# Second input projection, mLSTM cell and second output projection in one block of a two-part transformer kernel

## Chip, cores and metric

The kernel runs on one core of one Trainium2 chip. The metric is the device time of one execution in microseconds (us), as the median of several runs.

## The reference, cut to what matters

Two blocks follow each other on 256 tokens of width 2048, all in float32. The first (two kinds of attention) ends in `h`. The second starts with `layernorm`, then computes this, and ends with a mixture of experts over the result (`peer_ffn`), which is untouched here:

```python
proj = h @ w_in[l]
cB, cC, ch, q, k, v, o, gi, gf = jnp.split(proj, split_at, axis=-1)
y_conv = cB * causal_dwconv(cC * ch, conv_w[l], conv_b[l])
gates = (jnp.concatenate([gi, gf], axis=-1) + b_gate[l]).astype(jnp.float32)
logi = gates[..., :M_HEADS]
logf = jax.nn.log_sigmoid(gates[..., M_HEADS:])
hm = mlstm_chunkwise(hd(q), hd(k), hd(v), logi, logf)
hm = layernorm(hm, mh_norm_g[l].reshape(M_HEADS, M_HEAD_DIM), ...)
y_m = jax.nn.sigmoid(o) * hm.reshape(Bn, S, D_MLSTM)
mix = jnp.concatenate([y_conv, y_m], axis=-1) @ w_out[l]
h = layernorm(ALPHA * h + mix, ln1_g[l], ln1_b[l])
```

`cB`, `cC`, `ch`, `q`, `k`, `v`, `o` are 1024 wide each, `gi` and `gf` 8. The cell `mlstm_chunkwise` has 8 heads of width 128; for each it weighs `q k^T` by exponentials of the gates under a causal mask, multiplies with `v` and divides by a row sum.

## The kernel before

**Slabs.** Every weight matrix is read as slabs of 128 x 1024 float32 (512 KB). SP loads slab n into `raw[n % 4]` once slab n-4 has been split. ACT rounds it into `w_hi` (`round_slab`, L146, two halves of 512 columns), DVE writes the rest `w_lo = raw - w_hi` (`split_slab`, L153, two halves), and PE multiplies hi*hi, lo*hi and hi*lo (L162 to L164). `w_hi` and `w_lo` have two buffers each, so ACT may round a half of slab m once PE is through with that half of slab m-2. On ACT and on DVE the work of slab m+1 is written ahead of whatever belongs to slab m. `feature_slab` makes 24 products of 256 columns from a slab (features on the partitions), `token_slab` 12 of 512 columns (tokens on the partitions). Both wait on `lo_ready` for each half of their slab. Each engine runs its instructions in the order in which they are written; the engines meet only at semaphores.

**Three stages**, each a block of its own with a branch on every engine at its end (L64):

- The second input projection (from L1070): 8 transposes of `h` with rounding and splitting; 48 slabs for `cB`, `cC`, `ch`, six for each of 8 groups of 128 features, in a loop, with the convolution of a group as seven DVE instructions in a row (L1187 to L1199) behind the group's last split; 32 slabs for q and k in loops; the gate columns (L1114, L1118); then 32 slabs for v and o, written out without a loop for PE and ACT.
- The cell (from L1240): DVE, ACT and PE make the gates' running sums and maxima; GpSimd (POOL) copies each head's q and k into `qk` and multiplies `o2` with the norm's gain (L1254); then for each head PE makes the scores and the exponents' row (L1328, L1329, L1331), DVE masks (L1389, L1390), ACT takes exponentials (L1283 to L1285), DVE weighs (L1395), PE multiplies with v (L1341 to L1343), ACT copies the result out (L1290), DVE divides (L1407 to L1416). After the eighth head come the norm over all heads (L1428 to L1443), 16 transposes of `hm` (L1356), and their rounding and splitting into `mix_hi` and `mix_lo` (L1303, L1448). No slab is multiplied in this stage; SP loads none.
- The second output projection (from L1458): 32 slabs of `w_out_2`, `token_slab` in loops, with the residual sum after every 8 slabs (L1501), at the end the norm `norm_stats` (8 instructions L279) and `norm_apply` (L288, L289).

## Time and profile before

| | us |
|---|---|
| median of 3 runs | 3099.87 |
| lowest and highest | 3096.27, 3116.24 |
| the profiled execution, its own time | 3101.69 |
| its span in the trace | 3099.5 |

The profiled execution is 1.8 us above the median; 2.2 us lie outside its span. Over the span PE is busy 2911.5 us (94%), DVE 1670.1, ACT 1329.3, POOL 620.5. The three stages that are changed lie between 1013.6 and 1525.0 us of the span.

### The profile page before, as it was taken

How to read it: one execution, taken by the hardware profiler on the slowest of the kernel's cores; microseconds unless marked ns; L12 is line 12 of the kernel's file. 1: busy time of each engine (PE TensorE's matmuls, PEld its weight loads, DVE VectorE, ACT ScalarE, POOL GpSimd, SP SyncE). 2: the span in 40 equal slices, each digit the busy share in tenths (PEclk: the TensorE clock that was granted, in tenths of full speed). 3: DMA queues.
4: the chain of work that ended last, by engine and by line, in shares of the span. 5: the costliest groups of instructions: out<-in, count | busy, mean ns of one | idle time of the engine just before them, and what ended most of it. 6: DMA issues, size and time to landing. Idle time of an engine off the chain costs nothing.

```text
span 3099.5 us, 53380 instructions
## 1 busy us (share of the span) xinstructions
PE 2911.5 (94%) x16728; PEld 2535.3 (82%) x16728; DVE 1670.1 (54%) x3187; ACT 1329.3 (43%) x2492; POOL 620.5 (20%) x496
## 2 busy tenths in 40 slices
PE   8999998899887899987799999999999999999996
PEld 7987877888665899866699998888887888888885
DVE  3143245322456665446588875555555666666666
ACT  2132243322543444433344445555554555555553
POOL 1100001200000000010000187777751111111110
PEclk9999999999988899978899999999999999999998
DMA  7742355933343355424444567777767666666663
GB/s 271 276 135 89 96 164 159 366 102 98 102 150 135 138 189 191 167 83 157 160 166 175 176 176 184 185 188 185 185 192 249 215 216 218 219 218 218 215 214 131
DMA packets 182994, 554.19 MB, mean 179 GB/s; under 512 B 53776, under 2 KB 53808, under 8 KB 179600
## 3 DMA queue, kind: packets, MB, share of 16 engines
q1 hardware_dynamic: 136656, 500.25, 47.9%
q0 software_dynamic: 45696, 48.88, 7.2%
q10 hardware_dynamic: 576, 4.19, 0.3%
q8 instruction: 41, 0.67, 0.1%
q14 instruction: 25, 0.20, 0.0%
HBM read 532.13 MB, written 21.10 MB: 178 GB/s over the span
## 4 chain that ended last, share of the span: by engine, by line
PE 49%; DVE 1%; ACT 0%; issue 0%; ACTq 0%; DVEq 0%
PE PS L1706 11%; PE PS L162 11%; PE PS L163 10%; PE PS L164 10%; PE PS L1708 6%; PE PS L1677 0%; DVE stats L279 0%; DVE hb L1987 0%; PE PS L254 0%; DVE hb L289 0%; DVE hb L288 0%; DVE w_lo L153 0%; DVE wj_lo L1755 0%; DVE h L268 0%; ACT w_hi L146 0%
## 5 line engine op out<-in xcount | busy, mean ns | idle before, releaser
L153 DVE TENSOR_TENSOR w_lo<-raw,w_hi 128x512 fp32r<-128x512 f32 x1696 | 1177.8, 717 | 919.3 <-ACT w_hi L146 917.4
L146 ACT ACTIVATE w_hi<-raw 128x512 fp32r<-128x512 f32 x1696 | 1030.5, 629 | 924.0 <-PE PS L164 823.0
L1706 PE MATMUL PS<-h,w_hi 128*128 128x512 f32 x1504 | 533.1, 400 | 2.0 <-DVE w_lo L153 2.0
L1619 POOL DMA_INDIRECT g_dram<-gt,spot x256 | 418.1, 1633 | 454.4 <-DVE gt L1947 348.6
L1708 PE MATMUL PS<-h,w_lo 128*128 128x256 f32 x1504 | 423.2, 281 | 0.0
L162 PE MATMUL PS<-w_hi,wj_hi 128*128 128x512 f32 x1024 | 399.3, 390 | 4.3 <-DVE wj_lo L1755 4.3
L164 PE MATMUL PS<-w_hi,wj_lo 128*128 128x512 f32 x1024 | 398.8, 389 | 0.0
L163 PE MATMUL PS<-w_lo,wj_hi 128*128 128x512 f32 x1024 | 398.8, 389 | 0.0
L1706 PEld LDWEIGHTS PS<-h,w_hi 128*128 128x128 f32 x1504 | 283.4, 188 | 73.1 <-DVE w_lo L153 2.4
L1708 PEld LDWEIGHTS PS<-h,w_lo 128*128 128x128 f32 x1504 | 284.9, 189 | 0.0
L162 PE MATMUL PS<-h,w_hi 128*128 128x256 f32 x800 | 228.8, 286 | 5.0 <-DVE w_lo L153 2.9
L162 PEld LDWEIGHTS PS<-w_hi,wj_hi 128*128 128x128 f32 x1024 | 192.6, 188 | 45.0 <-DVE wj_lo L1755 3.9
L163 PE MATMUL PS<-h,w_hi 128*128 128x256 f32 x800 | 227.0, 284 | 0.0
L164 PE MATMUL PS<-h,w_lo 128*128 128x256 f32 x800 | 227.0, 284 | 0.0
L163 PEld LDWEIGHTS PS<-w_lo,wj_hi 128*128 128x128 f32 x1024 | 192.6, 188 | 39.9
L164 PEld LDWEIGHTS PS<-w_hi,wj_lo 128*128 128x128 f32 x1024 | 192.5, 188 | 40.1
L162 PE MATMUL PS<-x_hi,w_hi 128*128 128x256 f32 (+1 forms) x512 | 177.0, 346 | 22.5 <-ACTq L480 13.0
L1631 POOL TENSOR_TENSOR wt<-wt,pick 128x512 f32 (+1 forms) x64 | 82.6, 1291 | 533.0 <-PE PS L164 483.2
L162 PE MATMUL PS<-h_hi,w_hi 128*128 128x256 f32 x640 | 179.3, 280 | 4.2 <-DVE w_lo L153 2.5
L163 PE MATMUL PS<-h_lo,w_hi 128*128 128x256 f32 x640 | 178.2, 278 | 0.0
L164 PE MATMUL PS<-h_hi,w_lo 128*128 128x256 f32 x640 | 178.2, 278 | 0.0
L163 PE MATMUL PS<-x_lo,w_hi 128*128 128x256 f32 (+1 forms) x512 | 175.2, 342 | 0.0
(322 smaller groups left out, 4373.4 us busy)
## 6 DMA issues: line engine op xcount, KB each, us to landing
raw<-in_u_s SPq DMA_DIRECT2D x256, 512.0 KB, 4.1
raw<-in_v SPq DMA_DIRECT2D x256, 512.0 KB, 4.6
raw<-in_w_in_s SPq DMA_DIRECT2D x112, 512.0 KB, 3.6
raw<-in_w_mod_s SPq DMA_DIRECT2D x64, 512.0 KB, 4.6
raw<-in_w_in_a SPq DMA_DIRECT2D x64, 512.0 KB, 3.7
raw<-in_w_in_b SPq DMA_DIRECT2D x64, 512.0 KB, 3.7
raw<-in_w_out_s SPq DMA_DIRECT2D x64, 512.0 KB, 3.5
raw<-in_w_gate_s SPq DMA_DIRECT2D x32, 512.0 KB, 3.5
```

The costliest lines, as they stand in the source:

```text
L146: act.activation(w_hi[m % 2][:, half], raw[:, m % NRAW, half], ACT.Copy).then_inc(hi_ready, 1)
L153: dve.tensor_tensor(w_lo[m % 2][:, half], raw[:, m % NRAW, half], w_hi[m % 2][:, half].bitcast(F), ALU.subtract).then_inc(lo_ready, 1)
L162: pe.matmul(out, lhs[0], rhs[0], start=start, stop=False)
L163: pe.matmul(out, lhs[0], rhs[1], start=False, stop=False)
L164: return pe.matmul(out, lhs[1], rhs[0], start=False, stop=stop)
L1619: pool.indirect_dma_start(g_dram, bass.IndirectOffsetOnAxis(spot[:, t, h, k:k + 1], 0), gt[:, t, h, k:k + 1], None, compute_op=ALU.add).th ...
L1631: pool.tensor_tensor(two, two, pick[:, b, :].rearrange("p (j t) -> p j t", j=2), ALU.mult)\
L1706: pe.matmul(PS[:, 6 + j % 2, :], w_hi[m % 2][:, c], h_both[:, kk, :, :].rearrange("p a t -> p (a t)"), start=(kk == 0), stop=False)
L1708: last = pe.matmul(PS[:, 6 + j % 2, 0:T], w_lo[m % 2][:, c], h_hi[:, kk, :], start=False, stop=(kk == KT - 1))
```

## The change

The three stages become one block. The order of the slabs changes: q and k first (loops), then the gates, then v and o with the gates' running sums between their slabs, then the 48 convolution slabs, written out, and between them the cell, one head for each group of six slabs, then the output projection, written out. DVE's work for a group and a head is cut into pieces of one to six instructions, one behind each slab's split (`conv_first`, `conv_second`, `mask` with `conv_third`, `divide`, `weigh`, `centre`). The convolution's last two steps go to ACT (`mix_round`) and POOL (`mix_lo`); ACT also copies out `a_sb`. The scores read q and k straight from `q2` and `k2`, so POOL's copies are gone. The norm over a head's 128 values is taken head by head: `centre` subtracts the mean and multiplies with `o2` (now with the gain); the scale by the root of the variance is applied for all heads at once in the output projection, half on DVE, half on ACT. The output projection first takes, for three of the four column blocks, the slabs that need only the convolution's half of `mix` (12 slabs), and between its 9th and 11th slab come the 16 transposes of `hm`; then the other 12, then the 8 of the fourth block. The sums of the last norm are taken after each block of columns. ACT loads the table of Exp after the last o slab, and the table of Sqrt at the fifth output slab. `w_in_2` and `w_out_2` are laid out on the host in the new order; slabs, products and bytes are the same in number.

```diff
+        OUT2 = [(c, g) for c in range(3) for g in range(4)] + [(c, g) for c in range(3) for g in range(4, 8)] + [(3, g) for g in range(8)]
+        with stage() as blk:
+            @blk.sync
+            def _(sp):
+                load_slabs(sp, src_in2, base["in2"], NRAW, N_WIN2)
+                load_slabs(sp, src_out2, base["out2"], 0, NRAW)
+                load_slabs(sp, src_out2, base["out2"], NRAW, N_OUT2)
+                load_slabs(sp, src_wq, base["wq"], 0, NRAW)
+                sp.wait_ge(ready, 2)
+
+                sp.dma_start(h_dram, h_buf[:, :, :]).then_inc(h_stored, 16)
...
+                pool.wait_ge(par_in, 80)
+                pool.wait_ge(vo_free, 4)
+                pool.tensor_tensor(o2[:, :, :], o2[:, :, :], mh_g[:, None, :].broadcast_to([P, TT, WA]), ALU.mult).then_inc(o_gate, 1)
+                for e in range(HEADS):
+                    pool.wait_ge(mixed_hi, e + 1)
+                    pool.tensor_tensor(mix_lo[:, e, :], yc[:, e % 2, 1, :], mix_hi[:, e, :].bitcast(F), ALU.subtract)\
+                        .then_inc(mixed, 1)
+
+                pool.wait_ge(scores, HEADS)
+                for i, name in enumerate(("ln1_g", "ln1_b")):
+                    pool.dma_start(par[i][:, :], bcast(io[name])).then_inc(ln_in, 16)
```

PE between the v and o slabs, then heads beside slabs, then the output projection:

```diff
+                for c in range(4):
+                    if c >= 2:
+                        pe.wait_ge(vo_free, c - 1)
+                    for g in range(8):
+                        token_slab(pe, [PS[:, 2 * (c % 2) + t, :] for t in range(TT)], None, m0 + 32 + 8 * c + g, g, h_hi, h_lo)
+                        if (c, g) == (0, 4):
+                            pe.wait_ge(g_dve, 1)
+                            pe.wait_ge(acc_free, 2 * HEADS + 2)
+                            for a in range(2):
+                                for t in range(TT):
+                                    last = pe.transpose(PS[0:HEADS, 7, a * T + t * P:a * T + (t + 1) * P], lg[:, t, 4 * a, :], ident)
+                            last.then_inc(g_tr, 1)
...
+                def score(e):
+                    w = e % 2
+                    if e == 0:
+                        pe.wait_ge(vo_free, 4)
+                    if e >= 2:
+                        pe.wait_ge(wts, e - 1)
+                    q, k = q2[:, e, :], k2[:, e, :]
+                    pe.matmul(PS[:, w, 0:T], k[:, 0:P], q, start=True, stop=True)
+                    pe.matmul(PS[:, w, T:T + P], k[:, P:T], q[:, P:T], start=True, stop=True)
+
+                    pe.matmul(PS[:, 2 + w, 0:T], cst[0:HEADS, C_ONES:C_ONES + P], neg[:, e, :],
+                              start=True, stop=True).then_inc(scores, 1)
+
+                def weighted(e):
+                    w = e % 2
+                    pe.wait_ge(wts, e + 1)
+                    if e:
+                        pe.wait_ge(num_sb, e)
+                    v0, v1 = v2[:, 0, e, :], v2[:, 1, e, :]
+                    pe.matmul(PS[:, 4, 0:P + 1], ss[:, w, 0, :], v0, start=True, stop=True)
+                    pe.matmul(PS[:, 4, P + 1:2 * P + 2], ss[:, w, 1, :], v0, start=True, stop=False)
+                    pe.matmul(PS[:, 4, P + 1:2 * P + 2], ss[:, w, 2, :], v1, start=False, stop=True).then_inc(nums, 1)
+
+                for e in range(HEADS):
+                    for part, freed in enumerate((a_copied, c_copied, zed)):
+                        if e:
+                            pe.wait_ge(freed, e)
+                        for half in range(2):
+                            feature_slab(pe, PS[:, 5 + part, 0:T], None, mc + 6 * e + 2 * part + half, half, h_hi, h_lo, slice(0, T))
+                            if (part, half) == (0, 1):
+                                score(e)
+                    weighted(e)
...
+                pe.wait_ge(wts, HEADS)
+                bank = lambda c: [PS[:, 2 * c + t, :] for t in range(TT)]
+                for i, (c, g) in enumerate(OUT2):
+                    if c == 0 and g < 4:
+                        pe.wait_ge(mixed, 2 * g + 2)
+                    if (c, g) == (2, 0):
+                        pe.wait_ge(num_sb, HEADS)
+                        pe.wait_ge(a_copied, HEADS)
+                    if c < 3 and g >= 4:
+                        pe.wait_ge(cp_c, g - 3)
+                    if (c, g) == (3, 0):
+                        pe.wait_ge(cp_c, 4)
+                    token_slab(pe, bank(c), None, mo + i, g, mix_hi, mix_lo)
+                    if g == 7:
+                        pe.sem_inc(resid, 1)
+                    if i in (8, 10):
+                        pe.wait_ge(scaled, 2 * HEADS)
+                        pe.wait_ge(c_copied, HEADS)
+                        pe.wait_ge(zed, HEADS)
+                        for b in range(i - 8, i - 6):
+                            if b >= 2:
+                                pe.wait_ge(cp_c, b - 1)
+                            for k in range(2):
+                                for t in range(TT):
+                                    last = pe.transpose(PS[:, 6 + b % 2, (2 * k + t) * P:(2 * k + t + 1) * P],
+                                                        hm[:, t, 2 * b + k, :], ident)
+                            last.then_inc(tr_c, 1)
```

ACT and DVE:

```diff
+                act.preload_act_table(ACT.Exp)
...
+                for e in range(HEADS):
+                    for s in range(6):
+                        round_slab(act, None, mc + 6 * e + s + 1)
+                        if s == 0 and e:
+                            num_copy(e - 1)
+                        if s == 2:
+                            a_copy(e)
+                        if s == 3:
+                            exponentials(e)
+                            if e:
+                                mix_round(e - 1)
+                        if s == 4:
+                            c_copy(e)
+                for i in range(N_OUT2):
+                    round_slab(act, None, mo + i + 1)
+                    if i == 0:
+                        num_copy(HEADS - 1)
+                    if i == 2:
+                        mix_round(HEADS - 1)
+                    if i == 4:
+                        act.wait_ge(asked_c, 1)
+                        act.activation(hv[:, :, 3], hv[:, :, 2], ACT.Sqrt).then_inc(given_c, 1)
+                    if i == 6:
+                        act.wait_ge(recip_c, 1)
+                        for h in range(HEADS):
+                            n = HEADS + h
+                            act.activation(hm[:, 1, h, :], hm[:, 1, h, :], ACT.Copy, scale=hv[:, n, 4:5]).then_inc(scaled, 1)
```

```diff
+                def conv_first(e):
+                    u = e % 2
+                    y, t = yc[:, u, 0, :], taps(e)
+                    dve.wait_ge(c_copied, e + 1)
+                    wait_multiplied(dve, None, mc + 6 * e + 6)
+                    dve.tensor_tensor(z[:, u, 2:T + 2], c_sb[:, u, :], PS[:, 7, 0:T], ALU.mult).then_inc(zed, 1)
+                    dve.wait_ge(zed, e + 1)
+                    step(dve.tensor_scalar(y, z[:, u, 2:T + 2], t[2], t[3], ALU.mult, ALU.add))
+
+                def conv_second(e):
+                    u = e % 2
+                    y, t = yc[:, u, 0, :], taps(e)
+                    step(dve.scalar_tensor_tensor(y, z[:, u, 1:T + 1], t[1], y, ALU.mult, ALU.add))
+                    step(dve.scalar_tensor_tensor(y, z[:, u, 0:T], t[0], y, ALU.mult, ALU.add))
+
+                def conv_third(e):
+                    dve.wait_ge(a_copied, e + 1)
+                    if e >= 2:
+                        dve.wait_ge(mixed, e - 1)
+                    dve.tensor_tensor(yc[:, e % 2, 1, :], yc[:, e % 2, 0, :], a_sb[:, e % 2, :], ALU.mult).then_inc(conved, 1)
...
+                def divide(e):
+                    w = e % 2
+                    dve.wait_ge(num_sb, e + 1)
+                    d = num[:, w, :, P]
+                    step(dve.scalar_tensor_tensor(den[:, w, 0, :], d, -1.0, d, ALU.mult, ALU.max))
+                    step(dve.tensor_tensor(den[:, w, 1, :], den[:, w, 0, :], colb[:, :, 1, e:e + 1].rearrange("p t o -> p (t o)"), ALU.max))
+                    step(dve.reciprocal(den[:, w, 2, :], den[:, w, 1, :]))
...
+                        x = dve.tensor_scalar(hm[:, t, e, :], num[:, w, t, 0:P], den[:, w, 2, t:t + 1], None, ALU.mult)
+                    x.then_inc(hms, 1)
+                    dve.wait_ge(hms, e + 1)
...
+                def centre(e):
...
+                        x = dve.bn_stats(st[:, t, e, :], hm[:, t, e, :])
+                    step(x)
...
+                        x = dve.bn_aggr(hv[:, t * HEADS + e, 0:2], st[:, t, e, :])
+                    step(x)
...
                     for t in range(TT):
+                        x = dve.scalar_tensor_tensor(hm[:, t, e, :], hm[:, t, e, :], hv[:, t * HEADS + e, 0:1],
+                                                     o2[:, t, e * P:(e + 1) * P], ALU.subtract, ALU.mult)
+                    step(x)
+
+                for e in range(HEADS):
+                    for s in range(6):
+                        split_slab(dve, None, mc + 6 * e + s + 1)
+                        if e and s == 0:
+                            conv_first(e - 1)
+                        if e and s == 1:
+                            conv_second(e - 1)
+                        if s == 2:
+                            mask(e)
+                            if e:
+                                conv_third(e - 1)
+                        if e and s == 3:
+                            divide(e - 1)
+                        if s == 4:
+                            weigh(e)
+                        if e and s == 5:
+                            centre(e - 1)
+                e = HEADS - 1
+
...
+                    dve.wait_ge(resid, c + 1)
+                    wait_multiplied(dve, None, mo + 1 + (max(i for i, (cc, g) in enumerate(OUT2) if cc == c)))
+                    for t in range(TT):
+                        hh = h_buf[:, t, c * 512:(c + 1) * 512]
+                        x = dve.scalar_tensor_tensor(hh, hh, ALPHA, PS[:, 2 * c + t, :], ALU.mult, ALU.add)
+                    step(x)
+                    for t in range(TT):
+                        x = dve.bn_stats(stats[:, t, c, :], h_buf[:, t, c * 512:(c + 1) * 512])
+                    step(x)
+                for i in range(N_OUT2):
+                    split_slab(dve, None, mo + i + 1)
+                    if i == 0:
+                        conv_first(e)
+                    if i == 1:
+                        conv_second(e)
+                        conv_third(e)
+                    if i == 2:
+                        divide(e)
+                    if i == 3:
+                        centre(e)
+                        dve.tensor_scalar(hv[:, :, 2], hv[:, :, 1], 1e-5, None, ALU.add).then_inc(asked_c, 1)
```

**DVE in the convolution.** Before, one group's seven instructions stand in a row (the first five are here; ISA and REGISTER_ALU rows are steps of the sequencer between them; `z` is the product that is convolved, `yc` the sum, `cv` the taps):

```order
L1187 TENSOR_TENSOR z<-c_sb,PS 128x256
L1188 REGISTER_ALU
L1189 ISA
L1189 TENSOR_SCALAR yc<-z,cv 128x256
L1190 REGISTER_ALU
L1191 ISA
L1191 SCALAR_TENSOR_TENSOR yc<-z,cv,yc 128x256
L1192 REGISTER_ALU
L1193 ISA
L1193 SCALAR_TENSOR_TENSOR yc<-z,cv,yc 128x256
L1194 REGISTER_ALU
L1195 TENSOR_TENSOR yc<-yc,PS 128x256
```

Now the same work stands in pieces behind the splits (`x2` is one slab), with the cell's between them (`ee` exponents, `den` and `hm` the head's result):

```order
L153 TENSOR_TENSOR w_lo<-raw,w_hi 128x512 x2
L1412 TENSOR_TENSOR z<-c_sb,PS 128x256
L1414 TENSOR_SCALAR yc<-z,cv 128x256
L153 TENSOR_TENSOR w_lo<-raw,w_hi 128x512 x2
L1419 SCALAR_TENSOR_TENSOR yc<-z,cv,yc 128x256
L1420 SCALAR_TENSOR_TENSOR yc<-z,cv,yc 128x256
L153 TENSOR_TENSOR w_lo<-raw,w_hi 128x512 x2
L1431 TENSOR_TENSOR ee<-PS,cst 128x128
L1432 TENSOR_TENSOR ee<-PS,cst 128x128
L1426 TENSOR_TENSOR yc<-yc,a_sb 128x256
L153 TENSOR_TENSOR w_lo<-raw,w_hi 128x512 x2
```

Between two slabs' splits there are now at most six instructions, those of `centre`.

**PE in the cell.** Before, one head's products stand alone, in a loop over the heads:

```order
L34 ISA
L1325 REGISTER_ALU
L1328 MATMUL PS<-qk 128x256
L1329 MATMUL PS<-qk 128x128
L1331 ISA
L1331 MATMUL PS<-neg,cst 128x256
L1341 ISA
L1341 MATMUL PS<-v,ss 128x129
L1342 MATMUL PS<-v,ss 128x129
L1343 ISA
L1343 MATMUL PS<-v,ss 128x129
```

Now the scores of a head stand behind the second slab of its group, among the slabs' products (the three of L1200 to L1202, with `v`, stand behind the sixth slab):

```order
L162 MATMUL PS<-h_hi,w_hi 128x256
L163 MATMUL PS<-h_lo,w_hi 128x256
L164 MATMUL PS<-h_hi,w_lo 128x256
L1188 MATMUL PS<-q,k 128x256
L1189 MATMUL PS<-q,k 128x128
L1191 MATMUL PS<-neg,cst 128x256
L162 MATMUL PS<-h_hi,w_hi 128x256
L163 MATMUL PS<-h_lo,w_hi 128x256
```

The cell's products have moved from a stretch of their own to places between slabs.

**POOL.** Before, the product of `o2` with the gain (L1254) is taken in the cell's stage, where DVE splits no slab:

```order
L1241 UNCONDITIONAL_BRANCH
L60 ISA x14
L1244 DMA eye<-in_consts 8x8
L1245 DMA mh_g<-in_mh_g 128x1024
L1248 COPY qk<-q 128x256
L1249 COPY qk<-k 128x256
L1248 COPY qk<-q 128x256
L1249 COPY qk<-k 128x256
L1254 TENSOR_TENSOR o<-o,mh_g 128x2048
```

Now it stands in the one block, released by the copy of the last o slabs (`vo_free`), with eight small differences for `mix_lo` behind it:

```order
L1112 DMA eye<-in_consts 8x8
L1113 DMA mh_g<-in_mh_g 128x1024
L1114 MEMSET z 128x2x2
L1115 MEMSET v 128x16
L1119 TENSOR_TENSOR o<-o,mh_g 128x2048
L1122 TENSOR_TENSOR mix_lo<-yc,mix_hi 128x256 x8
L1127 DMA parb_6606<-in_ln_g 128x2048
L1127 DMA parb_6607<-in_ln_b 128x2048
```

POOL's product now falls beside the first convolution slabs.

## Rows read from the trace of the kernel before

**Rows 1.** Windows: busy us (count) of PE, PEld, DVE, ACT, POOL; PEclk; DMA; GB/s.

```profile
1349.00:1418.00 69.00, 36.45 (x122) 26.05 (x122) 40.41 (x153) 18.38 (x47) 11.71 (x19) 0.57 0.02 8
1418.00:1422.00 4.00, 4.00 (x10) 3.13 (x11) 1.94 (x3) 1.40 (x3) 1.11 (x2) 0.50 0.65 238
1422.00:1426.00 4.00, 4.00 (x17) 3.19 (x17) 1.43 (x3) 1.30 (x3) 0.00 (x0) 0.87 1.03 430
```

**Rows 2.** Timeline of PE around the cell: start, us, what, [idle before <- releaser].

```profile
1348.79 0.40 PE L164 MATMUL PS<-w_hi,h_lo 128*128 128x512 f32 x1
...
1411.14 1.97 PE L1356 MATMUL PS<-cst,hm 128*128 128x128 f32 x8 [14.25 <-DVE hm L1443]
...
1417.73 0.79 PE L162 MATMUL PS<-w_hi,mix_hi 128*128 128x512 f32 x1 [2.03 <-DVEq L1493]
```

**Rows 3.** Timeline of PE in the cell, same product of two heads; clock 0.50.

```profile
1378.51 1.06 PE L1328 MATMUL PS<-qk 128*128 128x256 f32 x2
...
1382.52 1.06 PE L1328 MATMUL PS<-qk 128*128 128x256 f32 x2
```

**Rows 4.** L1342 alone: duration in ns, min/median/max.

```profile
L1342 PE MATMUL PS<-v,ss x16: 275/422/422, 1373.6 to 1396.4; 128*128 x12, 128*128 128x129 f32 x4
```

**Rows 5.** The tile c_sb, one copy per group of six slabs.

```profile
L1143 ACT ACTIVATE c_sb<-PS x8: 366/366/366, 1041.7 to 1160.7; 128x256 f32<-128x256 f32 x8
```

**Rows 6.** Timeline around a group's end in the convolution, DVE and ACT.

```profile
1079.16 0.41 DVE L1187 TENSOR_TENSOR z<-c_sb,PS 128x256 f32<-128x256 f32 x1
...
1082.80 2.49 DVE L153 TENSOR_TENSOR w_lo<-raw,w_hi 128x512 fp32r<-128x512 f32 x4
...
1083.33 0.63 ACT L146 ACTIVATE w_hi<-raw 128x512 fp32r<-128x512 f32 x1 [0.73 <-PE PS L164]
...
1085.22 0.63 ACT L146 ACTIVATE w_hi<-raw 128x512 fp32r<-128x512 f32 x1 [1.26 <-PE PS L164]
```

**Rows 7.** Timeline of DVE in the cell, its last heads and the norm.

```profile
1391.21 0.16 DVE L1407 SCALAR_TENSOR_TENSOR den<-num 128x2 f32<-128x2 f32 x1 [1.52 <-ACT num L1290]
...
1392.03 0.48 DVE L1416 TENSOR_SCALAR hm<-num,den 128x128 f32 x2
...
1392.43 0.55 DVE L1395 SCALAR_TENSOR_TENSOR ss<-PS,ee 128x384 f32<-128x384 f32 x1
...
1398.46 3.19 DVE L1428 BATCH_NORM_STATS2 st<-hm 128x6 f32<-128x128 f32 x16
...
1403.66 4.29 DVE L1439 SCALAR_TENSOR_TENSOR hm<-hm,hv,o 128x128 f32<-128x128 f32 x16
```

**Rows 8.** Timeline of ACT in the o slabs and in the cell.

```profile
1325.15 1.28 ACT L1163 ACT_TABLE_LOAD   x1
...
1327.25 1.09 ACT L1163 ACTIVATE o<-PS 128x512 f32<-128x512 f32 x2 [0.81 <-PE PS L164]
...
1391.08 0.39 ACT L1283 ACTIVATE ee<-ee,colb 128x128 f32<-128x128 f32 x1
```

**Rows 9.** Timeline of POOL and DVE, in the cell and late in the expert part.

```profile
1356.86 4.75 POOL L1254 TENSOR_TENSOR o<-o,mh_g 128x2048 f32<-128x2048 f32 x1 [2.08 <-DMA mh_g<-in_mh_g]
...
2607.16 1.29 POOL L1631 TENSOR_TENSOR wt<-wt,pick 128x512 f32 x1 [8.26 <-PE PS L164]
...
2607.68 2.05 DVE L153 TENSOR_TENSOR w_lo<-raw,w_hi 128x512 fp32r<-128x512 f32 x2 [0.67 <-ACT w_hi L146]
```

**Rows 10.** Windows after a stall of PE in the expert part, columns as in Rows 1.

```profile
2374.00:2378.00 4.00, 2.25 (x5) 1.82 (x6) 2.76 (x3) 1.03 (x2) 3.27 (x4) 0.67 0.95 369
2378.00:2382.00 4.00, 4.00 (x17) 3.28 (x16) 1.72 (x3) 2.01 (x4) 0.60 (x2) 0.90 0.99 418
```

**Rows 11.** Timeline of the output projection's end, DVE and PE.

```profile
1507.67 1.28 DVE L1501 SCALAR_TENSOR_TENSOR h_buf<-h_buf,PS 128x512 f32 x2 [1.47 <-PE PS L164]
...
1508.99 2.47 DVE L279 BATCH_NORM_STATS2 stats<-h_buf 128x6 f32<-128x512 f32 x4
...
1525.03 1.30 PE L254 MATMUL PS<-cst,h_buf 128*128 128x128 f32 x5 [17.50 <-PEq L64]
```

655 lines of the change are left out of this document (249 added, 406 removed).

## Prediction

> **What bounds the kernel now.** Over the whole span PE is busy 94%, so I looked for the stretches where it is not, first in the slices, then in windows at the borders of stages. The cell's stage stands out [rows 1]: in 69 us PE is busy 36.5 us, at a mean granted clock of 0.57 of full speed, while DMA moves next to nothing (share 0.02). PE's timeline gives its exact length [rows 2]: the last product of the input projection begins at 1348.79 and runs 0.40 us, the first product of the output projection begins at 1417.73. So **68.5 us** pass between slab and slab. The reader should see two more things there. Before the 16 transposes PE waits 14.25 us for DVE's norm; and the cell's own products repeat every 4.01 us per head [rows 3] at clock 0.50, the lower of the two levels (1.2 GHz of 1.2 and 2.4), since PE had been nearly idle before them. Everywhere else in the three stages PE multiplies slabs back to back, so what bounds them outside the cell is PE, and inside the cell a chain of DVE, ACT and PE in turn.
>
> The change removes this stretch. Its worth is 68.5 us less what PE must still do for the cell, less the waits that the cell's work beside the slabs causes.
>
> **What PE still does.** (1) The six products of a head now stand among busy slabs, where I expect the full clock. Half of 4.01 us is 2.0 us. The single product L1342 shrinks less in the record, from 422 to 275 ns [rows 4], which would give 2.6 us, but starts follow each other faster than durations tell, so I take 2.1 us: 8 x 2.1 = **+17 us**, bounds 16 (half) and 32 (nothing gained by clock). (2) 16 transposes of `hm` and 8 small ones: eight take 1.97 us at the lower clock [rows 2], 24 at the full one 3 x 1.0 = **+3.0 us**.
>
> **What PE no longer loses.** (3) When the output projection starts, the clock is 0.50 for 4 us and 0.87 for 4 more [rows 1]: 2.0 + 0.5 = **-2.5 us**, since no pause precedes it now. (4) In the convolution DVE runs seven instructions in a row, from 1079.16 to 1082.80, 3.64 us [rows 6]. ACT, which rounds a half as soon as PE has freed it, then waits 1.26 us instead of 0.73: PE was 0.53 us late. Eight groups, eight copies [rows 5]: 8 x 0.53 = **-4.2 us**, if the pieces that take their place cause no wait. (5) The tail. After the last product DVE does the residual (1.28 us), then four `bn_stats` in 2.47 us, twice [rows 11]; six of the eight are now done earlier: 6 x 0.62 = 3.7, less about 0.2 for the root, which has no cover now: **-3.5 us**.
>
> **Whether the pieces fit beside the slabs.** The same event [rows 6] says how much room there is: 3.64 us of extra DVE work at one place cost PE 0.53 us, so about 3.1 us at one place cost nothing. The pieces: `conv_first`, `conv_second` and `conv_third` are five of the seven instructions, some 2.7 us in three places; the mask two instructions of the size of the pair that writes `hm` (0.48 us); `divide` from 1391.21 to 1392.03 and its pair 0.48, so 1.3; `weigh` 0.55 [rows 7]; `centre` two of `bn_stats` (3.19 / 16 = 0.2 each), two `bn_aggr`, two of the centring (4.29 / 16 = 0.27 each) [rows 7] and their waits, about 1.4. No place has more than 1.5 us. In sum 6.5 us per head; with 12 splits at 2.49 / 4 = 0.62 [rows 6] DVE works 14 us in a head. PE needs a group's period of (1160.7 - 1041.7) / 7 = 17.0 us [rows 5], less 0.53, plus 2.1: 18.6 us. DVE is at 75%, and PE stays the bound. ACT's largest piece is three exponentials and one rounding, 4 x 0.39 [rows 8] = 1.6 us, also under 3.1. In the output projection a residual is 1.28 + 2 x 0.62 = 2.5 us at one place [rows 11], ACT's eight scalings about 8 x 0.33 = 2.6, and the transposes' copies make ACT wait for PE and DVE for ACT, one slab ahead of need. These come close to the room, so I put down **+1.5 us**, between 0 and 6. The gates' sums between v and o slabs are pieces of 0.3 to 1.5 us: nothing, and their cover is the same room. SP's loads follow each other without a border; POOL's two more loads at the start are covered by the transposes.
>
> **The one place that does not fit.** After the last o slab (time 0) ACT copies out for 1.09 us and now loads the table of Exp, 1.28 us [rows 8] (the earlier load, for the sigmoid, ran while ACT waited anyway, as it began 2.1 us before its use). The next rounding ends 0.63 us later, at 3.0; DVE's half would be ready at 3.7, and PE, with a slab lasting (17.0 - 0.53) / 6 = 2.7 us, would wait 1.0 us. But the same copy releases POOL's product with the gain, 4.75 us long [rows 9]: it runs from about 1.1 to 5.9 us, and DVE's split would start at 3.0. In the trace a POOL tensor_tensor of 1.29 us starts at 2607.16, and two splits that start at 2607.68 need 2.05 us instead of 1.38 [rows 9]: the first ends where POOL's end (2608.45) plus one split would put it. So the split waits for the rest of the product: ready at 5.9 + 0.7 = 6.6, PE waits 6.6 - 2.7 = **3.9 us**. After a wait of that size PE's clock fell to 0.67 and 0.90 in two windows of 4 us [rows 10], which costs 1.3 + 0.4 = **+1.7 us**. Together +5.6 us. This is where a rule speaks against the change: the Trainium skill, "SBUF — State Buffer", section "Who interferes with whom", says that a VectorE instruction with two SBUF inputs and a GpSimd instruction that reads SBUF exclude each other, and the one that starts second waits for the whole of the first. By that rule the split is held for the whole rest, as I take it; if the trace's case were only a slowing by half, this term would be about 2 us. By the same rule each of the eight `mix_lo` products holds DVE for up to 0.6 us, which the room covers.
>
> **The sum.** -68.5 + 17 + 3.0 - 2.5 - 4.2 - 3.5 + 1.5 + 5.6 = -51.6 us. The profiled execution took 3101.69 us (span 3099.5 and 2.2 outside it), so its like would take 3050.1; it lay 1.8 above the median, so I forecast **3048 us** as a median. The terms' bounds (cell +15, output projection -1.5 to +4.5, the POOL wait -3.6 to +1, convolution 0 to +4) make 3042 to 3066.
>
> **Rivals.**
> A. *The cell's products are as dear as in the trace.* Then (1) is 32, not 17: 3063 us. For it: L1342's record shrinks only by a third, and its weights load at 0.33 us where a stationary operand changes with every product. Against it: the records' starts. 12 in 100.
> B. *Small waits in every group.* The room of 3.1 us was measured for one disturbance per group; now there is one behind each slab, DVE waits for ACT and ACT for DVE (mask, exponentials, weigh), and POOL holds DVE once a head. 1.5 us per head and some 4 in the output projection give 3048 + 12 + 4 = 3064 us. Against it: 75% load, and every wait is on work written at least half a slab earlier. 15 in 100.
> C. *Better than summed.* POOL's product finds DVE between splits or costs less, and straight code without the loops' branches runs the six slabs faster than 16.5 us per group: 3048 - 4 - 6 = 3038 us. 12 in 100.
> D. *Slower than before.* The mechanism: rounding, split and product have no lead left, so that all inserted work shows. Its place is the 48 convolution slabs and the output projection. Its price: DVE 8 x 6.5 = 52, ACT 8 x 2.7 = 22, residuals, scalings and copies in the output projection 22, together 96 us, against the gain of 52: 3144 us. It decides from the point where the lead of DVE over PE, 3.1 us now, falls to nothing; in the convolution before it was used up only once a group. 3 in 100.
>
> That the change does not do what it says is no case apart: the order of the instructions shows the cell's products between slabs.
>
> **How the numbers follow.** My forecast's own case, 3042 to 3056, has 58 in 100. The range takes in it, A, B and C: 3035 to 3067, which leaves out D and the far parts of A and B. About 1% (31 us) is what a measurement of this kernel can tell from no change. Faster by more than that is everything under 3069: 92 in 100; within 1% the tail of A and B together, 5; slower by over 1%, D, 3.
>
> **What the profile after should show.** PE without a pause between the last o slab and the last output slab, but for one wait of about 4 us beside POOL's product, with DVE's split beside it lasting some 3.6 us; the six products of a head within 2.0 to 2.6 us; copies into `c_sb` 18.6 us apart; no wait of PE for `w_lo` over 0.5 us elsewhere; the tail from the last product to the next stage 14 us instead of 17.5. The prediction is wrong if groups take over 19.5 us (then B or A, told apart by whether PE waits or multiplies), or if the clock is below 1.00 in the groups' windows.

## The result, and the profile after

| | median, us | lowest and highest |
|---|---|---|
| before | 3101.32 | 3096.27, 3116.24 |
| after | 3062.98 | 3052.07, 3065.07 |

The ratio is 0.9876, with a 95% interval of 0.9841 to 0.991: faster by 38.3 us, where the sum had said 51.6. The profiled execution of after is the fastest of the four, 3052.07 us (span 3050.4); the other three took 3061.65 to 3065.07.

The block is best measured from trace to trace, between two events that both kernels have: the first transpose of the second part, and the first transpose of the stage behind the block. Before, they stand at 1013.6 and 1525.03 [rows 11], 511.4 us apart. PE's timeline has the first of them here, before and after, and the second one of after behind the last product (start, duration, what, the idle time ahead and what ended it):

```profile
1013.61 1.94 PE L254 MATMUL PS<-cst,h_buf 128*128 128x128 f32 x8 [26.34 <-PEq L64]
1015.24 1.94 PE L254 MATMUL PS<-cst,h_buf 128*128 128x128 f32 x8 [26.36 <-PEq L64]
...
1471.39 0.39 PE L164 MATMUL PS<-w_hi,mix_lo 128*128 128x512 f32 x1
1485.55 1.73 PE L254 MATMUL PS<-cst,h_buf 128*128 128x128 f32 x7 [13.77 <-PEq L64]
```

From 1015.24 to 1485.55 that is 470.3 us, so the block is **41.1 us** shorter. The part ahead of it is 1.6 us longer, and the expert part behind it, which nobody touched, takes 1564.9 us instead of 1574.5. Those 9.6 us are no part of the change (see the last section); they are why this one execution is faster than its three siblings: 3052.07 + 9.6 = 3061.7, and the others took 3061.65 to 3065.07.

Now the pause. [Rows 1] and [rows 2] showed 68.5 us with hardly a product. The view of waits for PE, over the whole block of after (total, times, longest):

```profile
PE PS L254 <- PEq L64: 40.1, 2, 26.4
PE PS L162 <- DVE w_lo L153: 3.6, 1, 3.6
PE PS L254 <- DVE h_lo L268: 1.8, 3, 0.7
PE PS L162 <- DVE h_lo L268: 1.7, 1, 1.7
```

The first line is the two ends of the block (26.4 ahead of it, 13.7 behind), the last two are its first transposes. Between them **one** wait is left, 3.6 us. It is the one forecast beside POOL's product, and the timeline around it answers to [rows 9]:

```profile
1221.29 1.09 ACT L1284 ACTIVATE o<-PS 128x512 f32<-128x512 f32 x2 [2.09 <-PE PS L164]
1222.39 1.28 ACT L1286 ACT_TABLE_LOAD   x1
1222.53 4.54 POOL L1119 TENSOR_TENSOR o<-o,mh_g 128x2048 f32<-128x2048 f32 x1 [203.12 <-ACT o L1284]
1223.68 2.19 ACT L146 ACTIVATE w_hi<-raw 128x512 fp32r<-128x512 f32 x4
1224.42 5.00 DVE L153 TENSOR_TENSOR w_lo<-raw,w_hi 128x512 fp32r<-128x512 f32 x4 [4.49 <-ACT w_hi L146]
1227.67 0.58 PE L162 MATMUL PS<-h_hi,w_hi 128*128 128x256 f32 x1 [3.56 <-DVE w_lo L153]
```

The reader should see the order: ACT's copy ends at 1222.4 and releases POOL; ACT has the first half rounded at 1224.3; DVE's split starts at 1224.42, but POOL works until 1227.07, and PE gets its `w_lo` at 1227.67, which is POOL's end and one split later. The clock follows. Windows (busy us of PE, PEld, DVE, ACT, POOL, granted clock, DMA share, GB/s), first the wait, then the middle of the convolution, then the gates:

```profile
1222.60:1226.60 4.00, 1.52 (x13) 1.31 (x11) 2.18 (x1) 3.26 (x5) 4.00 (x1) 1.00 0.14 56
1226.60:1230.60 4.00, 2.93 (x13) 2.93 (x14) 2.82 (x4) 0.00 (x0) 0.47 (x1) 0.50 0.22 56
1230.60:1234.60 4.00, 4.00 (x20) 3.43 (x18) 1.38 (x2) 1.53 (x3) 0.00 (x0) 0.64 0.54 206
1240.00:1380.00 140.00, 140.00 (x1129) 136.45 (x1129) 97.56 (x215) 68.97 (x137) 5.21 (x7) 1.00 0.53 164
1120.70:1124.70 4.00, 4.00 (x37) 4.00 (x35) 1.20 (x2) 2.82 (x4) 0.00 (x0) 0.94 0.48 132
1124.70:1128.70 4.00, 4.00 (x21) 4.00 (x20) 0.09 (x1) 0.00 (x0) 0.00 (x0) 0.50 0.48 135
1128.70:1132.70 4.00, 4.00 (x17) 3.71 (x18) 1.12 (x8) 0.00 (x0) 0.00 (x0) 0.50 0.00 0
```

The fourth row is the heart of the change: 140 us in which PE never stands still, at the full clock (2.4 GHz), with DVE at 70%. And yet the groups are late. The tile `c_sb`, one copy per group as in [rows 5]:

```profile
L1298 ACT ACTIVATE c_sb<-PS x8: 365/366/367, 1241.2 to 1377.0; 128x256 f32<-128x256 f32 x8
```

(1377.0 - 1241.2) / 7 = **19.40 us** per group, where 18.6 was forecast; that is just inside the sign of being wrong, 19.5. As PE does not wait, its products themselves must be slower. Their starts tell it; durations don't, for each is 0.28 in both kernels. After, at the end of head 1's slabs:

```profile
1245.70 0.28 PE L164 MATMUL PS<-h_hi,w_lo 128*128 128x256 f32 x1
1245.83 0.28 PE L162 MATMUL PS<-h_hi,w_hi 128*128 128x256 f32 x1
1245.94 0.28 PE L163 MATMUL PS<-h_lo,w_hi 128*128 128x256 f32 x1
1246.07 0.28 PE L164 MATMUL PS<-h_hi,w_lo 128*128 128x256 f32 x1
1246.19 0.39 PE L1200 MATMUL PS<-v,ss 128*128 128x129 f32 x2
```

Before, in the convolution:

```profile
1060.77 0.28 PE L164 MATMUL PS<-h_hi,w_lo 128*128 128x256 f32 x1
...
1061.11 0.28 PE L164 MATMUL PS<-h_hi,w_lo 128*128 128x256 f32 x1
...
1061.45 0.28 PE L164 MATMUL PS<-h_hi,w_lo 128*128 128x256 f32 x1
```

Three products take 0.34 us before and 0.36 to 0.37 after: 0.1133 and 0.120 each over longer stretches. A group has 144 of them, so 19.40 - 144 x 0.120 = **2.12 us** are left for a head's six products of the cell. Read directly from PE's starts they take (1246.78 - 1246.07) + (1253.98 - 1252.49) less two steps of 0.12, 1.96 us, and behind each of the two places one step between slab products is some 0.1 us longer. That term was right (2.1). The whole excess is in the slabs, and it is not in the new code alone: the q and k loops, whose code did not change, run at 0.120 too. The 512-column products of the output projection kept their pace (0.2267 before, 0.2268 after). Those of the v and o slabs became a little faster, 0.2289 before and 0.2270 after over the last 96 of them; experiments 4 to 7 come back to this.

The transposes of `hm` stand in the output projection at full clock, 1.03 and 1.04 us for eight (1.97 before, [rows 2]), without a wait:

```profile
1407.24 1.03 PE L1238 MATMUL PS<-cst,hm 128*128 128x128 f32 x8
```

The tail on DVE answers to [rows 11]: the residual as before, then two statistics instead of four, with the root's small steps in the open behind them.

```profile
1471.88 1.28 DVE L1492 SCALAR_TENSOR_TENSOR h_buf<-h_buf,PS 128x512 f32<-128x512 f32 x2 [1.43 <-PE PS L164]
1473.20 1.29 DVE L1495 BATCH_NORM_STATS2 stats<-h_buf 128x6 f32<-128x512 f32 x2
```

PE's pause at the end is 13.77 us instead of 17.50.

### The profile page after: what moved, and what is told of

The parts are those of the page before. It is cut to its first block, busy times and chain, and to the rows that moved or that the text cites. A ratio compares the mean times of both kernels' runs of the same rounds, so it can differ in the third digit from the quotient of the medians.

```text
span 3050.4 us, 52640 instructions
## 1 busy us (share of the span) xinstructions
PE 2893.8 (95%) x16728; PEld 2537.8 (83%) x16728; DVE 1663.1 (55%) x3163; ACT 1338.5 (44%) x2517; POOL 620.3 (20%) x488
## 4 chain that ended last, share of the span: by engine, by line
PE 49%; DVE 1%; ACT 0%; issue 0%; ACTq 0%; DVEq 0%
PE PS L1727 11%; PE PS L162 11%; PE PS L163 11%; PE PS L164 11%; PE PS L1729 6%; PE PS L1698 0%; DVE stats L279 0%; DVE hb L2008 0%; PE PS L254 0%; DVE hb L289 0%; DVE hb L288 0%; DVE w_lo L153 0%; DVE wj_lo L1776 0%; DVE h L268 0%; ACT h L262 0%
## 5 line engine op out<-in xcount | busy, mean ns | idle before, releaser
L1727 PE MATMUL PS<-h,w_hi 128*128 128x512 f32 x1504 | 521.6, 391 | 2.0 <-DVE w_lo L153 2.0
L1727 PEld LDWEIGHTS PS<-h,w_hi 128*128 128x128 f32 x1504 | 281.3, 187 | 63.4 <-DVE w_lo L153 2.4
```

The source lines that it names most:

```text
L1727: pe.matmul(PS[:, 6 + j % 2, :], w_hi[m % 2][:, c], h_both[:, kk, :, :].rearrange("p a t -> p (a t)"), start=(kk == 0), stop=False)
```

## The experiments

Twelve more kernels ran. A ratio is to the kernel before, run beside each. All times of a block below go from transpose to transpose as above; where PE's path is the same, two kernels agree in it to 0.1 us (470.3 twice, 458.5 twice, below), which no total does.

**1 and 2. Where `h_hi` lies.** The likeliest cause of slower products in unchanged code was that the buffers had moved. In the programs' layout `h_hi`, the operand that streams through PE as 256 columns (1024 bytes per partition and feature tile), starts at byte 117312 of a partition before and at 84352 after. Both kernels were given 64 unused bytes ahead of it.

```diff
+        gap = buf2("gap", [P, 16])
         h_hi = buf2("h_hi", [P, KT, T], R)
```

> The changed kernel with 64 bytes left free ahead of h_hi, so that h_hi and h_lo start at an odd multiple of 64 bytes, as in the kernel before (117312), instead of a multiple of 128 (84352). In the changed kernel the products of 256 columns follow each other every 0.120 us, in the kernel before every 0.1133 us, in loops and in straight code alike. Theory 1 (the start address of the operands h_hi and h_lo sets the pace): 0.1133 us again, copies into c_sb 18.4 us apart instead of 19.4, and 24 x 80 x 0.0067 = 13 us less for the kernel. Theory 2 (something else in the merged block, such as its length, slows the products): 0.120 us stays, no difference in time.

> The kernel before with 64 bytes left free ahead of h_hi, which then starts at a multiple of 128 bytes. Theory 1 (start address): the 80 slabs of 256-column products slow from 0.1133 to 0.120 us per product, copies into c_sb 17.9 us apart instead of 17.0, the kernel some 13 us slower. Theory 2 (the merged block): no difference, 17.0 us and the same time.

The changed kernel with the gap: 3056.36 us, ratio 0.987 (0.9838 to 0.9902); block 464.6 us, 5.7 less than after; groups 18.93 us apart, products 0.116 to 0.118 us. So the pace moved, but not to the 0.1133 us that was expected of any odd multiple of 64. The kernel before with the gap: 3104.38 us, ratio 1.0017 (0.9989 to 1.0044); its groups lie 17.57 us apart instead of 17.00:

```profile
L1144 ACT ACTIVATE c_sb<-PS x8: 367/367/367, 1047.8 to 1170.8; 128x256 f32<-128x256 f32 x8
```

and its products 0.120 us apart, as in after. The expectation had 17.9 us for the groups. They are shorter because the slower products use up the wait for DVE that each group of the kernel before ends with: 17.00 - 144 x 0.1133 = 0.68 us are outside the products before, 17.57 - 144 x 0.120 = 0.29 us with the gap. So a shift of 64 bytes, with nothing else changed, makes the products of the kernel before as slow as those of after. The total hides it, which is why the block and the groups are the measure here.

**3. Back to the old place.** 192 bytes (`[P, 48]`) put `h_hi` at 84544, which is 576 modulo 1024 as before the change.

> The changed kernel with 192 bytes left free ahead of h_hi, so that h_hi starts at 84544, which is 576 above a multiple of 1024, as in the kernel before (117312). So far: start at a multiple of 128 gave 0.120 us per 256-column product in four profiles of four; 64 bytes further gave 0.1177. Theory 1 (the pace hangs on the start address beyond the step of 128 bytes): 0.1133 us, copies into c_sb 18.4 us apart, the kernel 8 us faster than with the gap of 64. Theory 2 (any odd multiple of 64 gives a pace that wanders between 0.1133 and 0.118): 18.4 to 19.1 us, uneven within the run as with the gap of 64.

3054.0 us, ratio 0.984 (0.98 to 0.9879); block **458.5 us**, 11.8 less than after. The groups:

```profile
L1299 ACT ACTIVATE c_sb<-PS x8: 367/367/368, 1236.6 to 1366.6; 128x256 f32<-128x256 f32 x8
```

18.57 us apart: the prediction's 18.6 to the tenth, while the expectation had 18.4. And 511.4 - 458.5 = 52.9 us, where the sum of the prediction was 51.6. Starts in PE's timeline of this kernel, to be held against the two fences above:

```profile
1245.22 0.28 PE L164 MATMUL PS<-h_hi,w_lo 128*128 128x256 f32 x1
...
1245.56 0.28 PE L164 MATMUL PS<-h_hi,w_lo 128*128 128x256 f32 x1
...
1245.90 0.28 PE L164 MATMUL PS<-h_hi,w_lo 128*128 128x256 f32 x1
```

**4 to 7. Which places are fast.** Four kernels with other gaps, each run once: 128, 320 and 448 bytes in the changed kernel, 256 in the one before.

> The changed kernel with 128 bytes of gap: h_hi begins at 84480, 0 modulo 256 (before the gap: 128). If odd multiples of 64 are what is fast, this one is as slow as no gap: 19.4 us between copies into c_sb, block 470 us. If the place modulo 256 counts with four values of its own, 0 may give another.

> The changed kernel with 320 bytes of gap: h_hi begins at 84672, 192 modulo 256 as with the gap of 64 bytes, but 704 modulo 1024 instead of 448. If the place modulo 256 sets the pace: the value between the two, as with 64 bytes: copies 18.93 us apart, block 464.6 us. If the place modulo 1024 does: any other value, 18.6 or 19.4 us the likeliest.

> The changed kernel with 448 bytes of gap ahead of h_hi, which then begins at 84800: the same place modulo 256 (64) as the gap of 192 bytes and as the kernel before, another one modulo 512 and 1024 (832). If the place modulo 256 sets the pace: copies into c_sb 18.6 us apart, 256-column products 0.113 us apart, the block from its first transpose to the next stage's 458.5 us. If only the place modulo 1024 that the kernel before had (576) is fast: 19.4 us, 0.120 us, 470 us.

> The kernel before with 256 bytes of gap ahead of h_hi, which moves it from 117312 to 117568: 64 modulo 256 as it was, 832 instead of 576 modulo 1024. If the place modulo 256 sets the pace, nothing changes: copies into c_sb 17.0 us apart, block 511.4 us. If any move of the buffer slows the products: 17.57 us and 516.3 us, as with 64 bytes.

| kernel | gap, bytes | `h_hi` starts at | modulo 256 | between groups, us | block, us |
|---|---|---|---|---|---|
| after | 0 | 84352 | 128 | 19.40 | 470.3 |
| after | 64 | 84416 | 192 | 18.93 | 464.6 |
| after | 128 | 84480 | 0 | 19.24 | 468.9 |
| after | 192 | 84544 | 64 | 18.57 | 458.5 |
| after | 320 | 84672 | 192 | 18.93 | 465.8 |
| after | 448 | 84800 | 64 | 18.59 | 458.5 |
| before | 0 | 117312 | 64 | 17.00 | 511.4 |
| before | 64 | 117376 | 128 | 17.57 | 516.3 |
| before | 256 | 117568 | 64 | 17.11 | 507.7 |

In the changed kernel the place modulo 256 orders the groups of all six: 64 is the fastest, and the same at two distances; 192 lies between, again the same twice; 0 and 128 are slow. Modulo 512 and 1024 the two fast ones differ (64 and 320, 576 and 832), so that is not it. The blocks at 192 differ by 1.2 us, nearly all of it ahead of the gates; their groups do not. The kernel before fits: at 64 again, with 256 bytes, its groups are 0.1 us longer at most, against 0.57 with 64 bytes. The blocks of these two kernels don't differ from before by the slabs alone, though. In the cell's stage the clock came back earlier in both kernels with a gap than in before: L1342 repeats every 4.01 us at clock 0.50 and, with 256 bytes, from 1391 us on as here:

```profile
1391.57 0.49 PE L1342 MATMUL PS<-v,ss 128*128 x2
1393.71 0.49 PE L1342 MATMUL PS<-v,ss 128*128 x2
```

That is 2.14 us per head, at clock 0.96 from 1391 to 1395 us, and it made the pause between slab and slab 62.5 us with the gap of 256 and 65.3 with that of 64, against 68.5. Less this, the rest of the block is 2.3 us longer with 256 bytes and 8.1 with 64. Of each, 1.7 us are the clock at the gates (experiment 11); up to the gates the 80 slabs take 226.0 us in before, 226.9 with 256 bytes and 234.3 with 64, of which faster v and o slabs (below) give some back. These rows are also the answer to rival A out of the old kernel itself: a head's products at full clock take half of 4.01. The totals hide all this: the four single times are 3058.91, 3049.93 and 3064.86 us (128, 320 and 448 bytes) and 3096.34 us, and the longest of the first three belongs to the shortest block.

The v and o slabs answer to the place as well, in another order. There `h_hi` and `h_lo` are the stationary operands, and the products have 512 columns. 96 of these products, up to the last o slab, take 21.79 us in after and 22.39 us with the gap of 64 (first and last start; the first two rows are after, the others the kernel with the gap):

```profile
1199.07 0.39 PE L164 MATMUL PS<-w_hi,h_lo 128*128 128x512 f32 x1
1220.86 0.39 PE L164 MATMUL PS<-w_hi,h_lo 128*128 128x512 f32 x1
1195.14 0.39 PE L164 MATMUL PS<-w_hi,h_lo 128*128 128x512 f32 x1
1217.53 0.40 PE L164 MATMUL PS<-w_hi,h_lo 128*128 128x512 f32 x1
```

Per product that is 0.2270 us at 128 modulo 256, the fastest place here and the slowest above; the others measure 0.2290 at 64, 0.2325 at 0 and 0.2333 at 192, and kernels at the same place agree to 0.0002. Of the four places the block is shortest at 64 because the 80 slabs weigh more. From after to the gap of 192 bytes the q and k slabs go from 95.0 to 90.1 us (up to the first product of the gates), the convolution's stretch from 161.5 to 153.9 (up to the first output slab), 12.5 us less in all, and the stretch between, with v and o, from 100.3 to 100.9, 0.7 more. The output projection reads `mix_hi` and `mix_lo`, which lie ahead of the gap at byte 51584 in both kernels; its products keep 0.2267 to 0.2269 in every run.

What was not told apart: a gap moves every buffer behind it. The buffers of the weights don't move, so `h_hi` and `h_lo` are the only operands of the slabs' products that do; which of the two makes the pace, and why, is open.

**8. POOL's product by heads.** The product with the gain, one instruction of 4.54 us, becomes eight of 0.74 us, each released by the scores of its head.

```diff
-                pool.tensor_tensor(o2[:, :, :], o2[:, :, :], mh_g[:, None, :].broadcast_to([P, TT, WA]), ALU.mult).then_inc(o_gate, 1)
                 for e in range(HEADS):
+                    pool.wait_ge(scores, e + 1)
+                    o_e = o2[:, :, e * P:(e + 1) * P]
+                    pool.tensor_tensor(o_e, o_e, mh_g[:, None, e * P:(e + 1) * P].broadcast_to([P, TT, P]), ALU.mult).then_inc(o_gate, 1)
...
```

> The changed kernel with POOL's product of o2 and the gain cut into eight, one head's 128 columns each, taken in turn with the eight mix_lo products. Theory 1 (DVE's split is held until POOL's instruction ends): PE's wait of 3.6 us at the first convolution slabs shrinks to 0.9 us, which ACT's table load leaves, the clock stays at 1.00, and about 4.5 us are gained; eight pieces of 0.6 us hold DVE without a wait of PE. Theory 2 (the wait comes from ACT's copy and table load): the wait stays near 3.6 us and the time is the same.

3046.43 us, ratio 0.9833 (0.9806 to 0.9861); block 465.3, 5.0 less than after. Timeline and windows of this kernel at the place of the wait:

```profile
1224.59 2.50 DVE L153 TENSOR_TENSOR w_lo<-raw,w_hi 128x512 fp32r<-128x512 f32 x4 [4.50 <-ACT w_hi L146]
1225.34 0.39 PE L162 MATMUL PS<-h_hi,w_hi 128*128 128x256 f32 x1 [1.05 <-DVE w_lo L153]
```

```profile
1225.00:1229.00 4.00, 3.66 (x28) 3.55 (x28) 2.78 (x5) 2.17 (x5) 0.00 (x0) 1.00 0.40 127
1229.00:1233.00 4.00, 4.00 (x31) 3.60 (x30) 1.80 (x4) 1.19 (x4) 0.74 (x1) 1.00 0.76 261
```

The wait falls from 3.56 to 1.05 us (the prediction's 1.0 for ACT's copy and table load alone), and the clock stays at 1.00. So POOL's product costs 2.5 us of waiting and 2.5 of clock. After a pause of 1.05 us the clock did not fall, after one of 3.56 it did.

**9. The output slabs in plain order.** The transposes stand behind the fourth output slab, as the order by columns needs them there; ACT's and DVE's work on `hm` moves forward with them.

```diff
-        OUT2 = [(c, g) for c in range(3) for g in range(4)] + [(c, g) for c in range(3) for g in range(4, 8)] + [(3, g) for g in range(8)]
+        OUT2 = [(c, g) for c in range(4) for g in range(8)]
...
-                    if i in (8, 10):
+                    if i == 3:
...
```

> The changed kernel with the 32 output slabs in plain order (column block by column block, all eight slabs of each), the 16 transposes of hm behind the fourth slab. Theory 1 (the order by what is ready hides the end of the cell): PE waits once, behind the fourth output slab, for centre, Sqrt, scaling, transposes, rounding and splitting of the cell's half, some 9 us, and loses 2 us more to the clock: 11 us slower than the changed kernel. Theory 2 (the order is of no weight, since DVE and ACT are ahead anyway): under 2 us.

3069.64 us, ratio 0.9909 (0.9882 to 0.9937); block 478.5, **8.2 more** than after. PE and ACT there:

```profile
1404.04 2.44 ACT L1343 ACTIVATE hm<-hm,hv 128x128 f32<-128x128 f32 x8 [0.32 <-DVE hv L1509]
1406.54 1.97 PE L1238 MATMUL PS<-cst,hm 128*128 128x128 f32 x8 [5.03 <-ACT hm L1343]
1409.07 1.97 PE L1238 MATMUL PS<-cst,hm 128*128 128x128 f32 x8 [0.56 <-DVE mix_lo L1516]
```

```profile
1405.00:1409.00 4.00, 1.97 (x8) 1.56 (x8) 1.38 (x5) 2.54 (x8) 0.00 (x0) 0.50 0.75 310
1409.00:1413.00 4.00, 3.93 (x16) 3.39 (x17) 2.08 (x4) 1.39 (x4) 0.00 (x0) 0.64 0.00 0
```

5.0 + 0.6 us of waiting and the lower clock behind it, less than the 11 us expected. The new order hides the last heads' norm and scaling, and buys a fifth of what the whole change brings.

**10. More work for DVE.** One 128 x 512 `tensor_tensor` more behind each of the 48 convolution slabs, to see how near DVE is to being late.

```diff
                         split_slab(dve, None, mc + 6 * e + s + 1)
+                        step(dve.tensor_tensor(spare[:, :], cst[:, 0:512], cst[:, 0:512], ALU.add))
```

> The changed kernel with one more DVE tensor_tensor of 128x512 (0.69 us, its result unused) behind each of the 48 convolution slabs' splits. Theory 1 (PE bounds the groups and DVE has 25% to spare): DVE's work per group rises from 14 to 18.3 us, still under 19.4; no wait of PE, copies into c_sb 19.4 us apart, the same time. Theory 2 (the chain of rounding, splitting and multiplying has used up its lead): PE waits at the places with the largest pieces, 0.5 to 0.7 us each, 2 to 4 us per group, 15 to 30 us in all.

3056.84 us, ratio 0.9855 (0.9823 to 0.9888); block 470.3, groups 19.40 us apart: nothing at all. 120 us of its convolution in one window, and of after:

```profile
1260.00:1380.00 120.00, 120.00 (x968) 116.95 (x967) 107.18 (x229) 59.95 (x121) 5.20 (x7) 1.00 0.53 162
```

```profile
1240.00:1360.00 120.00, 120.00 (x968) 116.95 (x968) 83.80 (x184) 58.85 (x118) 4.46 (x6) 1.00 0.53 164
```

DVE at 89% instead of 70%, and PE makes the same 968 products in 120 us. Rival B, small waits in every group, is refuted.

**11. The gates' products spread.** The 64 products for the gate columns, 16 and 32 columns wide, stood together behind the k slabs. Here they come in four parts behind the first four v slabs, and what follows from them four slabs later.

```diff
+                        if c == 0 and g < 4:
+                            gate_products(g)
-                        if (c, g) == (0, 4):
+                        if (c, g) == (1, 0):
                             pe.wait_ge(g_dve, 1)
```

> The changed kernel with the gates' 66 narrow products cut into four parts, one behind each of the first four v slabs, and the gates' sums on DVE, ACT and PE four slabs later. Theory 1 (the clock falls because the narrow products stand together; beside slabs it holds, as it did for the cell's): the two windows of 4 us at 0.50 and the one at 0.78 disappear, the products take 8.5 us instead of 11, and the block is 5 to 6 us shorter. Theory 2 (parts of 2 us are enough to lower the clock): it falls four times instead of once and nothing is gained, or a few us lost.

3054.82 us, ratio 0.9847 (0.9812 to 0.9881); block 465.3, 5.0 less than after. The first of these products starts at 1132.53 us. Two windows over them, all others up to 1154 us reading 1.00 as well:

```profile
1130.00:1134.00 4.00, 4.00 (x26) 3.53 (x25) 1.55 (x3) 3.86 (x6) 0.00 (x0) 1.00 0.42 126
1134.00:1138.00 4.00, 4.00 (x25) 3.47 (x25) 1.68 (x4) 1.26 (x2) 0.00 (x0) 1.00 0.61 218
```

In after the clock stood at 0.50 for two windows at the same work. It did so before the change as well: 0.72, 0.50 and 0.92 in three windows, about 3.4 us lost, against 5.1 after. Nor do the other 1.7 us belong to the change, since the kernel before with a gap of 64 bytes loses 5.1 us too, and so it does with 256:

```profile
1270.00:1274.00 4.00, 4.00 (x22) 4.00 (x21) 0.00 (x0) 0.00 (x0) 0.00 (x0) 0.53 0.21 85
1274.00:1278.00 4.00, 4.00 (x12) 3.23 (x12) 0.52 (x5) 0.63 (x1) 0.00 (x0) 0.50 0.00 0
1278.00:1282.00 4.00, 4.00 (x14) 3.15 (x13) 1.37 (x2) 0.99 (x2) 0.00 (x0) 0.69 0.00 0
```

Eleven of the twelve profiles in which these products stand together lose 5.1 us; the one of before is the exception, for which no run gives a reason. The 5 us were there to be had all along.

**12. All of it.** The gap of 192 bytes, POOL's product by heads, the gates spread, and the table of Exp loaded behind the second convolution slab instead of ahead of the first.

> The changed kernel with the gap of 192 bytes, POOL's product cut by heads, the gates' products spread and the table of Exp loaded behind the second convolution slab's rounding. If the effects add: 12 us or less for the pace, 6 for POOL's product, 5 for the gates, 1 for the table, together up to 24 us under the changed kernel, near 3040 us. If the gap does nothing: near 3050 us.

**3040.78 us**, ratio 0.9798 (0.9763 to 0.9833), the fastest of all; block 448.2 us. PE has no wait left between its first transposes and the end of the block, the one of 1.05 us included. The parts add up: 470.3 - 11.8 - 5.0 - 5.0 = 448.5. The table's late load, which took away the last wait, brought at most a few tenths.

## Why the prediction was right, and where it was not

The time after, 3063, is within the range and 15 us above the forecast. By the prediction's own terms, in us of the block:

| term | forecast | measured | from |
|---|---|---|---|
| the pause | -68.5 | -68.5 | no pause left |
| (1) a head's six products | +17 | +17.0 | 8 x 2.12 |
| (2) 24 transposes | +3.0 | about +3 | 1.03 and 1.04 for eight |
| (3) reheating | -2.5 | -2.5 | no pause ahead of the output slabs |
| (4) convolution's waits | -4.2 | -5.4 | 8 x 0.68 before (experiment 2), none after |
| (5) tail | -3.5 | -3.7 | 13.77 for 17.50 |
| output projection | +1.5 | 0 | no wait |
| POOL's product, wait and clock | +5.6 | +6.1 | 3.56 + 2.5 |
| pace of the slabs | none | +11.8 | gap of 192 bytes: 12.5 less 0.7 |
| clock at the gates | none | +1.7 | windows of both; not due to the change |
| sum | -51.6 | -40.5 | block: -41.1 |

0.6 us of the last line are not accounted for.

**What failed.** The step is "PE needs a group's period of (1160.7 - 1041.7) / 7 = 17.0 us [rows 5], less 0.53, plus 2.1: 18.6 us", and with it every slab that the sum costed at nothing because only its place in the order changes. It carried the duration of a slab over from the old trace, and the change moved the buffers: laying out one block's buffers in place of three stages' shifted `h_hi` from 64 to 128 modulo 256. 80 slabs x 24 products x 0.0067 us = 12.9 us; the gap takes 12.5 of them away and gives 0.7 to the v and o slabs, 11.8 in all. With the old place modulo 256 the same steps come to 458.5 against a forecast of 511.4 - 51.6 = 459.8 for the block. This cause is shown by a gap that makes the old kernel's products slow and by one that makes the new kernel's fast. What in the chip ties the pace to the place is open.

**The other misses.** The fall of the clock at the gates was nowhere in the prediction, which looked for the clock only behind waits; here it falls while PE is busy with narrow products. It is in both kernels, so it costs the sum only the 1.7 us that the one profile of before was spared. What PE lost at the end of a convolution group was 0.68 us and not 0.53. The range's upper end doesn't follow from the bounds listed: 3048 + 15 + 4.5 + 1 + 4 is 3072, not 3066. The output projection's 1.5 us, taken as a middle between 0 and 6, was 0. The clock behind POOL's product cost 2.5 us, not 1.7: the window taken from the expert part [rows 10] followed a stall, too, but its dip was shallower, 0.67 and 0.90 against 0.50 and 0.64.

**What held.** The place, the cause and the size of the only wait (3.56 us, forecast 3.9) came from two rows of the old trace [rows 9]: a split that had to sit out a POOL instruction. Here the trace decides between the two readings left open there, since the split ended one split's length behind POOL's end. The page "SBUF — State Buffer", section "Who interferes with whom", of the Trainium skill has it so, and this case's 3.56 us agrees; with POOL's instruction out of the way 1.05 us are left. The room on DVE was larger than argued: 75% was forecast, 70% measured (73% with the gap of 192, in 120 us of the faster groups), and 89% still cost nothing. The order of the output slabs holds 8.2 us of the gain. Of the rivals, A is refuted by 2.12 us per head, although its price, 3063 us, is the very time that was measured: a coincidence. B is refuted by the missing waits and by the added work, D with B. C's reasons fail as well: POOL's product held DVE in full, and, written out, the slabs of the convolution run at the pace of the q and k loops in the same kernel, 0.120 both.

That the time fell within the range is owed in part to its width, which rivals A and B had set. The profiled execution alone, 3052, would have looked like a near hit at 3050, by a 9.6 us difference in code that the change doesn't touch. Only the block's own length shows that 10 us are missing there.

## What to carry to other kernels

A duration carried over from an old trace holds only if the operands stay where they are: after a change that adds, removes or reorders buffers, compare the starts of successive products in code that did not change before explaining the rest, and try a gap of 64, 128 and 192 bytes ahead of the streaming operand. Measure a change from one fixed event to another inside the trace; the totals of one kernel scatter by 6 to 27 us here, while blocks with the same path of PE agreed to 0.1. In this kernel work laid beside slabs cost what PE itself must do for it, as long as each piece was shorter than the lead of the engine that feeds PE; look for the one instruction on a neighbouring engine that is longer than that lead, and cut it.

## What the runs showed of the hardware

- **The pace of a product depends on where its operand starts.** 256-column products followed each other in 0.1133 us with `h_hi` at 64 modulo 256, in 0.116 to 0.118 at 192, in 0.119 at 0, and in 0.120 at 128, 6% more. It isn't load on the other engines: the kernel with 128 had DVE at 70% and a DMA share of 0.53, the faster one with 64 had 73% and 0.55. Durations in the records stay at 0.28. Products of 512 columns, where `h_hi` and `h_lo` are the stationary side, rank the places otherwise: 0.2270 at 128, 0.2290 at 64, 0.2325 at 0, 0.2333 at 192.
- **PE at full occupancy lost its clock.** At the gates PE was busy 4.00 of 4.00 us in each window, with products 16 and 32 columns wide, and its granted clock went from 0.94 to 0.50, the lower level (1.2 GHz). The same products with a slab of 512-column products between each 16 or so kept it at 1.00.
- **The same code ran at two paces.** From the first transpose behind the block to the end of the span, nothing differs between the kernels. It took 1574.0 to 1575.8 us in before, with gaps of 64, 128, 192 and 448 bytes in after, with the product split, in plain order and in the best version, but 1564.2 to 1566.3 in after, with the DVE load, with the gates spread, with the gap of 320 and in the kernel before with 64 bytes, and 1560.0 in the kernel before with 256. It is spread over the expert part's slabs. In 100 us of it, the records of its 512-column products last 399 ns on average in before (L1706) and 391 in after (L1727).

  With one profile of each kernel it can't be told whether a kernel or an execution has its pace. The four times of after (3052.07, then 3061.65 to 3065.07) speak for the execution. What sets it is open.
